# An encoder trunk on one core: VectorE's order in the attention loop, three filler matmul groups, GpSimd's sums and the first identity turns are rearranged

## The reference, cut to what matters

```python
q, k, v = split(rmsnorm(x) @ w_qkv)             # 8 heads, q and k in two halves of 64, v of 128
q, k = rope(rmsnorm(q)), rope(rmsnorm(k))
p = softmax(q_half @ k_half.T / 8)              # two maps per head, m = 0, 1
a = p[0] - lam * p[1]                           # the mix
o = rmsnorm(a @ v) * (1 - lambda_init)
x = x + o @ w_o
x = x + square(relu(rmsnorm(x) @ w1)) @ w2      # then the pooling layer and its MLP
```

## Time and profile before

| | |
|---|---|
| median of 3 runs | 976.98 us (975.72 to 977.26) |
| the profiled execution | 976.44 us, its span 974.7 us |
| granted TensorE clock | full in all 40 slices of the page |
| busy of the span | TensorE 99%, VectorE 86%, ScalarE 49%, GpSimd 38% |
| chain that ended last | TensorE 93%, VectorE 5%, ScalarE 1% |
| attention loop | about 78 to 261 us of the span |

### The profile page before, as it was taken

The page is one execution under the profiler, slowest core; times in us unless marked ns, Lnnn a source line. Parts: engine busy times, 40 slices in busy tenths (PEclk is TensorE's granted clock), DMA queues, the critical chain, the costliest instruction groups (busy, mean ns, idle before and its releaser), DMA issues.

```text
span 974.7 us, 12899 instructions
## 1 busy us (share of the span) xinstructions
PE 965.4 (99%) x4652; PEld 793.0 (81%) x4652; DVE 839.2 (86%) x1141; ACT 474.3 (49%) x759; POOL 367.9 (38%) x325
## 2 busy tenths in 40 slices
PE   8999999999999999999999999999999999999998
PEld 7887777777888788888888887988888888888887
DVE  6696888989679999999989878789798988989883
ACT  5435656777566344453444543565445344453520
POOL 6851353224471827548624001541350513305000
PEclk9999999999999999999999999999999999999999
DMA  7243210200432433333333150303332333322202
GB/s 265 88 108 97 77 64 4 87 1 23 130 109 67 130 124 96 104 88 116 108 101 108 66 192 2 130 5 126 106 111 86 111 105 96 121 87 87 86 1 87
DMA packets 50967, 90.13 MB, mean 92 GB/s; under 512 B 8268, under 2 KB 9560, under 8 KB 50904
## 3 DMA queue, kind: packets, MB, share of 16 engines
q1 hardware_dynamic: 45456, 89.14, 29.1%
q10 hardware_dynamic: 5448, 0.17, 0.3%
HBM read 87.20 MB, written 2.10 MB: 92 GB/s over the span
## 4 chain that ended last, share of the span: by engine, by line
PE 93%; DVE 5%; ACT 1%; issue 1%; DMA 0%; ACTq 0%; DVEq 0%
PE pair L1735 45%; PE bank L1735 44%; PE pair L1798 1%; PE bank L1798 1%; DVE s_nmax L1375 1%; PE bank L1753 1%; DVE s_acc L1569 0%; DMA s_x_nat<-in_x 0%; DVE s_acc L1493 0%; PE bank L2109 0%; ACT s_p L998 0%; DVE s_w_lo L1225 0%; DVE s_p L1393 0%; PE bank L1810 0%; PE pair L2097 0%
## 5 line engine op out<-in xcount | busy, mean ns | idle before, releaser
L792 POOL TENSOR_TENSOR s_lt<-s_lbB,s_lbB 128x1024 f32<-128x1024 f32 x14 | 33.6, 2400 | 259.4 <-PE pair L1735 160.2
L1252 DVE TENSOR_TENSOR s_lbB_lo<-s_lbB,s_b_hi 128x1024 fp32r<-128x1024 f32 x64 | 124.6, 1967 | 5.7 <-ACT s_b_hi L893 3.4
L1225 DVE TENSOR_TENSOR s_w_lo<-s_raw,s_w_hi 128x1024 fp32r<-128x1024 f32 x72 | 118.3, 1662 | 4.4 <-ACT s_w_hi L871 3.1
L893 ACT ACTIVATE s_b_hi<-s_lbB 128x1024 fp32r<-128x1024 f32 x64 | 67.2, 1053 | 82.2 <-POOL s_lbB L792 39.8
L1735 PE MATMUL pair<-s_hT_hi,s_w_hi 128*128 128x512 f32 x256 | 100.3, 392 | 0.7 <-DVE s_w_lo L1225 0.7
L1735 PE MATMUL bank<-s_hT_hi,s_w_hi 128*128 128x512 f32 x256 | 100.2, 392 | 0.0
L1735 PE MATMUL pair<-s_hT_lo,s_w_hi 128*128 128x512 f32 x256 | 99.6, 389 | 0.0
L1735 PE MATMUL pair<-s_hT_hi,s_w_lo 128*128 128x512 f32 x256 | 99.6, 389 | 0.0
L1735 PE MATMUL bank<-s_hT_hi,s_w_lo 128*128 128x512 f32 x256 | 99.6, 389 | 0.0
L1735 PE MATMUL bank<-s_hT_lo,s_w_hi 128*128 128x512 f32 x256 | 99.6, 389 | 0.0
L1084 ACT ACTIVATE s_u_raw<-s_u_raw 128x512 f32<-128x512 f32 x64 | 40.4, 632 | 111.2 <-DVE s_u_raw L1460 111.2
(11 more groups left out here) (272 smaller groups left out, 2676.8 us busy)
## 6 DMA issues: line engine op xcount, KB each, us to landing
s_raw<-in_mlp_w SPq DMA_DIRECT2D x64, 512.0 KB, 3.8
s_lbB<-in_mlp_w SPq DMA_DIRECT2D x64, 512.0 KB, 3.3
s_raw<-in_attn_w_qkv SPq DMA_DIRECT2D x24, 512.0 KB, 4.1
s_raw<-in_attn_w_o SPq DMA_DIRECT2D x8, 512.0 KB, 3.3
s_x_nat<-in_x SPq DMA_DIRECT2D x4, 512.0 KB, 6.6
out<-s_acc SPq DMA_DIRECT2D x7, 256.0 KB, 2.0
s_raw<-in_pool_w SPq DMA_DIRECT2D x4, 256.0 KB, 2.8
out<-s_acc SPq DMA_DIRECT2D x2, 128.0 KB, 1.8
```

The costliest lines, as they stand in the source:

```text
L792: g.tensor_tensor(w2_raw[n][:], w2_raw[one][:], w2_raw[two][:], ALU.subtract).then_inc(t_done, 1)
L893: a.activation(b_hi[home][:], w2_raw[n][:], ACT.Copy).then_inc(w2_hi_done, 1)
L1225: v.tensor_tensor(w_lo[slot][:, cols], raw[k][:], f32(w_hi[slot][:, cols]), ALU.subtract)\
L1252: v.tensor_tensor(w2_lo[n][:], w2_raw[n][:], f32(b_hi[home][:]), ALU.subtract).then_inc(w2_lo_done, 1)
```

## The change

It does four things. (1) In VectorE's loop the factor and the mix of step i-1 move from behind the maxima of step i to ahead of them, right behind the reciprocal. (2) Of the product with w_o, column block 0 does head 0 in step 18, head 1 in step 19 and head 2 in step 21 (were: heads 0 and 1 in 18, head 2 in 20); block 1 does head 0 in step 19, heads 1 and 2 in step 21 (were: 0 and 1 in 19, 2 in 21). (3) GpSimd's sums on x wait for the mix of the step before, two of them come one and two steps later, and in block 1 the first weight difference waits for the first rest of w1. (4) Three identity turns are added before x's first tile, and nine instead of two stand before its second.

```diff
 W_O_PARTS = (
-    ((18, (0, 1)), (20, (2,)), (22, (3,))),
-    ((19, (0, 1)), (21, (2,)), (22, (3,))),
+    ((18, (0,)), (19, (1,)), (21, (2,)), (22, (3,))),
+    ((19, (0,)), (21, (1, 2)), (22, (3,))),
...
-X_SUMMED = (18, 18, 19, 22, 25, 26, 29, 30)
+X_SUMMED = (18, 19, 21, 22, 25, 26, 29, 30)
...
                 for c in range(NC):                                   # GpSimd, step i
+                    if i in (X_ADDED[c], X_SUMMED[c]) and i <= STEPS:
+                        pool.wait_ge(a_done, i)
...
                     if not first(b):                                  # GpSimd, w2_sum, T1
                         pool.wait_ge(y_ready, y_at(b - 1) + 2 * P3 + 2)
+                    if b == 1:
+                        pool.wait_ge(w_lo_done, 4 * w1_slab(b) + 1)
...
                 if 1 <= i <= STEPS:                                   # VectorE, step i
                     mix_root(i - 1)
+                    mix_factor(i - 1)
+                    combine(i - 1)
                 if i < STEPS:
                     maxima(i)
...
-                if 1 <= i <= STEPS:
-                    mix_factor(i - 1)
                 if 2 <= i < STEPS + 2:
                     turn_lo("map", i - 2)
-                if 1 <= i <= STEPS:
-                    combine(i - 1)
...
+            keep_turning(3)                                           # TensorE, start
             turn_in(0)
...
-            keep_turning(2)
+            keep_turning(9)
             turn_in(1)
```

## The result

The changed kernel takes 980.02 us (median of 6 runs, 979.56 to 980.88) against 976.08 us for the kernel before (6 runs, 975.67 to 977.26): 1.0037 times as long, interval 1.0027 to 1.0047. The forecast was 979.8. The profiled execution took 979.95 us, its span 978.2, which is 3.5 above the span before. Its mean granted clock is 1.000, as in three others of the six; in the remaining two, the longest (980.72 and 980.88 us), it is 0.998.

A forecast was written before the change was run, and what follows sets the result against it. TensorE has work in 965.4 of 974.7 us, so only its idle and slow places could move the time. Mix +4.4, sums 0, block 1 -0.9, start -0.7 gave +2.8 us, forecast 979.8 us, range 975.5 to 982.0.

The forecast's parts named there:

- The mix ahead of the maxima: Attention steps 18 to 28: factor and mix before the maxima make the attention part 4.4 us longer.
- The price per step (0.97): Steps following a side turn (q, k or o copy): maxima start 0.97 us later, 2.58 instead of 1.61 after E.
- the loop of 4.71: Exponentials, side copy, side rest, maxima, exponentials: E to E grows from 3.74 to 4.71 us in steps after a side turn.
- E: The end of a step's second exponential on ScalarE, from which the prediction counts the start of the maxima.
- the walk: Step-by-step forecast of when scores start in steps 19 to 28, ending with step 28 at 233.45 instead of 229.05 us.
- x's sums behind the mix: GpSimd's sums wait for the mix: worth 0.5 of VectorE's time at steps 17 to 19, price 0 (-0.5 to +0.3).
- The wait in block 1: GpSimd's first difference waits for the first w1 rest, removing TensorE's wait there: -0.9 us (-0.9 to +0.5).
- In time: Block 1: the second rest of w1, due at 323.9, would end about 323.2 despite colliding with the second difference.
- The start: Added identity turns before x's first two tiles may bring the clock's rise earlier: -0.7 us, within -1.8 to +1.1.
- Rival 1: Faster, 972.7 us: the mix fills VectorE's idle time before the maxima and TensorE's four waits go; chance 0.14.
- Rival 2: Reorder costs only about 2 us because ScalarE's copy and the rest come earlier; 976.8 us; chance 0.22.
- Rival 3: The clock's rise stays, so the identity turns cost 1.1 us; +4.6, 981.6 us; chance 0.10.

The follow-up runs named there:

- e1: The kernel before with only the factor and mix of step i-1 moved ahead of the maxima of step i; 985.32 us, ratio 1.0091.
- e5: The changed kernel with VectorE's rest of the side turn behind the mix instead of ahead of the reciprocal; 976.14 us, ratio 0.9995.
- e8: The kernel before with the moved mix and new filler parts, old steps of x's sums, no GpSimd waits, old start; 984.55 us, ratio 1.0082.
- e10: The kernel before with the moved mix, x's sums' new steps and their GpSimd waits; old parts and start, no block 1 wait; 981.12 us, ratio 1.0054.
- e11: e1 with the side turns of steps 21 and 25 made three times to keep TensorE busy; 984.85 us, ratio 1.0091 to the kernel before.
- e2: The changed kernel with the factor and mix back behind the maxima, all other parts kept; 974.60 us, ratio 0.9981 to the kernel before.
- e3: The kernel before with the added identity turns alone (3 before x's first tile, 9 instead of 2 before the second); 975.90 us, ratio 0.9998.
- e4: The kernel before with only the block 1 wait (GpSimd's first weight difference waits for the first rest of w1); 975.42 us, ratio 0.9993.
- e6: The kernel before with the new filler parts and new steps of x's sums, without GpSimd's waits, in the old order; 976.39 us, ratio 0.9995.
- e12: e2 with step 18's side copy ahead of the value copy, the value's rest behind step 19's maxima, and two w_o heads moved earlier; 973.99 us.

## Why the prediction was right, point by point

**The mix ahead of the maxima: +4.4 forecast, 4.6 to 4.9 measured in the trace.** The price per step (0.97) and the loop of 4.71 hold. Maxima minus E is 2.65, 2.60, 2.66, 2.60 and 2.60 us in steps 21, 22, 25, 26 and 27, where 2.58 was written. Maxima to E is 2.14. The starts of steps 19 to 28, counted from 141 us, are -0.20, 1.44, 0.97, 2.18, 2.20, 2.71, 2.71, 3.46, 3.47 and 4.63 late; the walk had 0.07, 1.59, 1.14, 2.31, 2.11, 2.67, 2.63, 3.40, 3.42 and 4.40. Near 167 us the changed kernel gains 0.3, and from there to step 28 it loses 4.9. The 0.3 too belongs to the moved mix: step 14 takes 6.11 us in all six kernels with the mix ahead of the maxima (after, e1, e5, e8, e10, e11), and 6.40 to 6.43 before and in e2, e3, e4, e6 and e12. Two of the lengths in the prediction's list are misread: by its own rule step 21 has 2.5, not 2.7, and step 22 has 5.05, not 4.9. Neither moves the sum, because the loop of 4.71 sets the starts of steps 22 and 24. e2 gives 5.4 for the mix from the timed side, and e5 shows the mechanism: with the same instructions and the side rest behind the mix, 3.9 of it are gone.

**x's sums behind the mix: 0 forecast; right only within this walk.** The walk's prices for the mix (0.66) and the factor (0.15) were taken from a mix with nothing over it. That is true only because of the waits on GpSimd. The step as I put it, "Worth 0.5 of VectorE's time at steps 17 to 19", missed that in the new order the mix is in the loop and so are its collisions. In e1 the maxima start 5.20, 3.66 and 3.66 us after the last exponential in steps 18, 21 and 25, in e10 3.80, 2.61 and 2.65: 3.5 us, nearly all of the 3.7 by which the traces differ. The forecast had the two right only as a pair: +4.4 and 0, where the runs have +9.3 for the mix by itself and about -4 for the waits and the sums' new steps.

**The moved parts.** Without a price of their own beyond the walk. Alone they do nothing (e6), and beside the moved mix 0.8 at most, which is not told apart from nothing (e8 against e1). From e10 (981.12) to the changed kernel (980.02) parts, start and block 1 together give 1.1; in the traces 0.85 of it lie in steps 20 and 21, where e10 has its slow stretch and the changed kernel has none.

**The wait in block 1: -0.9 forecast, 0.7 in the trace, 0.6 in e4 and within its interval.** The 0.9 came off as written, with the first rest at 1.21 us. TensorE did not wait for the second rest, so "In time" held for it; what failed is that nothing behind it was priced. I did not look at the third and fourth rests, which collide too and push VectorE's later work, for which TensorE waits at 345 us. The same wait, 0.54 us, stands in e4 at 339.83, and the kernel before has none there.

**The start: -0.7 forecast, nothing measurable (e3, 0.9998).** I chose -0.7 inside -1.8 to +1.1. At 12 us the gain was 1.70 against the trace, near the far end. At 57 and 72 us TensorE meets VectorE's projection and rotation work, which does not come earlier (its weight rests start at 55.01 before and 54.90 after), and 0.52 are left (0.36 in e3). What failed is that I worked the gain out at 10 us and didn't ask what is late next, which needed the slack of VectorE at 57 us.
The earlier trace rows are also one run, and a late one. Over the thirteen profiled executions the turns of x's third tile start at 11.26 to 11.88 with the new start (six) and at 11.86 to 12.95 with the old (seven), 0.85 earlier on average; at the turn near 72 us the averages are 71.54 and 71.78, and 0.24 are left. VectorE's weight rests start at 54.83 to 55.06 in six of the thirteen and at 54.00 to 54.27 in seven, under either start, and the two waits of TensorE at 57 and 72 us stand only in the three with the new start and the late rests (after, e3, e12). What sets VectorE's time there was not looked for.
The Trainium skill ("TensorE: Matmul & The Clock Gate", "What's actually happening") says that the number of slow matmuls at the start varies between runs of one kernel. The traces agree: with the same old start the third tile is turned at 12.95 before and at 11.94 in e4, where the first projection matmuls from 9.40 on are already 0.24 us apart and before they are still 0.43 apart.

**The sum.** By the trace: start -0.4, the mix near 167 us -0.3, attention from there +4.9, block 1 -0.7, together +3.5, as the spans have it; the medians have 3.9, and +2.8 was forecast. The median came within 0.3 us because the median of before that I started from (976.98) was 0.9 above its median of more runs (976.08), which covered most of the missing 1.1. That part is luck.

**The rivals.** Rival 1 (faster) needed the side rest to be done before the scores end; the 0.57 of idle time before that rest, with the mix behind it, shows that it was not. Even in e5's order, which takes that obstacle away, the mix ahead of the maxima is no gain: e5 takes 1.5 us more than e2, which has it behind them. Rival 2 (a cost of 2) is out: e2 against the changed kernel gives 5.4, and in the trace the side rest comes only 0.09 us earlier behind E (0.88 against 200.78 - 199.81 = 0.97). Rival 3 (the start loses) is out: the rise came early.

## What to carry to other kernels

When an instruction is moved ahead in an in-order engine, look at what stands before its new place and waits: the mix went behind a rest that waits for ScalarE, and so its time was added to the loop; ahead of that rest it would have filled the wait. A collision that costs little off the loop costs its whole length on it (here 1.4, 1.0 and 1.0 us in three steps), so price an edit that only separates two engines together with the edit that makes the operation critical. Follow a gain at the start until the next engine that keeps its own time, and read the start in more than one execution; a wait removed in one place came back here twice as a smaller one some tens of microseconds later.

## What the runs showed of the hardware

- VectorE and GpSimd, both with two inputs in SBUF, hold each other up in both directions: a rest of 1.21 us takes 3.33 or about 3.1 (9.35 for three), the mix 1.73 instead of 0.75, a factor of one column 0.57 instead of 0.15, and GpSimd's difference 3.38 and 3.20 instead of 2.40. The maxima, which read PSUM, take 1.28 with a GpSimd sum under them (step 18 of the changed kernel) and 1.27 without one. The Trainium skill ("GPSIMD Engine Reference", "Key points") says that VectorE instructions with two SBUF inputs contend with GpSimd for their interfaces; the traces agree and add the sizes.
- Inside a loop that keeps TensorE busy otherwise, waits of 2.65 and 1.95 us (e1), 2.13 and 1.97 (e8) and 1.85 (e10, before 196.69) were followed by 4 us stretches with the granted clock at 0.57 to 0.81. Waits of 1.85 (e1 before 199.17 and e11 before 198.18), 1.87 (the changed kernel), 1.76 (e11) and 1.70 (e8) were not. Length alone does not decide it, and it changes between runs of one kernel: the mean clock is 0.998 in three and 1.000 in two of e10, and 0.998 in two and 1.000 in four of the changed kernel. The two slow stretches of e1 lengthened their steps by 2.8 us and cost 1.15 net.
- The page's clock row shows full clock at the start, where 128-column turns are 0.24 us apart; the durations tell the level there, the row does not.
